# A two-layer decoder step: fewer page copies ahead of a weight load, one sum two tiles later, and a feed stage's first instructions reordered

## The chip, the cores and the metric

The kernel runs on one core of a Trainium2 chip. The metric is the device time of one execution in microseconds, as the median of several runs. The engines are PE (the matrix engine, with its weight loads as PEld), DVE (vector), ACT (activation), POOL (GpSimd) and SP, which issues most of the transfers.

## The reference, cut to what matters

Two layers of a decoder for a prompt group (16 meta tokens and 1024 prompt tokens) and a sample group (8 sequences of 4 tokens with 2048 past positions in a paged cache). The width is 1024.

```python
for i in range(2):
    n_p, n_s = rmsnorm(hp, norm_mix[i]), rmsnorm(hs, norm_mix[i])
    if i == 0:   # latent attention, 8 heads
        c_past = cache_kv_latent[0, page_table]     # 8 x 16 pages of 128 x 256
        kp_past = cache_k_rope[0, page_table]       # 8 x 16 pages of 128 x 64
        y_p = mla_output(mla_prompt_attend(...), w_kv_b, w_o)
        y_s = mla_output(mla_sample_attend(..., c_past, kp_past), w_kv_b, w_o)
    else:        # RWKV-7 time mixing
        y_p, y_s = rwkv7_time_mix(...)
    hp, hs = hp + y_p, hs + y_s
    hp = hp + sq_relu_mlp(rmsnorm(hp, norm_ffn[i]), ffn_w_up[i], ffn_w_down[i])
    hs = hs + sq_relu_mlp(rmsnorm(hs, norm_ffn[i]), ffn_w_up[i], ffn_w_down[i])

def rmsnorm(x, g):
    return x * rsqrt(mean(x * x) + eps) * g
```

## The kernel before, in words

The program is written engine by engine, each with its instructions in a fixed order; semaphores are counted. Activations lie with the features on the partitions, as `hT` (8 tiles of 128 features by 1072 tokens). Products in full precision are made of rounded high parts and remainders: ACT rounds an operand to its `hi` part, POOL (for weights) or DVE (for activations) subtracts to get the `lo` part, and PE multiplies hi by hi, hi by lo and lo by hi.

**Attention over the prompt, and the page copies (about 116 to 492 us).** The eight heads are worked in four pairs. Each pair has its own query and key-value weights in the tiles `wq`, `wqp` and `wkv`, which the next pair overwrites. When PE has made its last use of a pair's weights, in the second head, it raises `wkv_used` behind a drain (line 943); after the last scores of that head it waits for the next pair's weights on `wq_s` (the raw queries of the next pair). SP issues these weights in `load_pair` (three transfers of `mla_w_q_b`, one of `mla_w_kv_b`, line 1823). SP also copies the 128 pages of the cache that the page table names into the scratch tensor `past_scratch`, one page for each turn of a loop (`gather`, line 1873): it reads the page's number, computes addresses and issues two transfers. Ahead of the weights of pairs 2, 3 and 4 and behind the last stand 32 such copies each. The sample attention, which begins after the four pairs, reads the scratch tensor and waits for all 128.

**The start of each feed stage (about 651 to 790 us, and 2413 to 2565 us).** The tokens are in four quarters of 268. PE makes the output product of the mixer, tile by tile (8 tiles a quarter, in `added`, each into one of four banks of the ring BV), DVE adds each tile to `hT` (`adds`, line 3316) and so empties the bank. For the norm, ACT squares a quarter (`squares_at`, line 2710), POOL folds its eight tiles of squares into one (`fold`, lines 2184 and 2186), PE sums over the partitions with a matrix of ones (`sums_at`), ACT takes the root (`deviations_at`, line 2716), DVE takes the reciprocal (`roots`, line 3586) and scales (`scaled`, line 3593, eight instructions). The fourth quarter's squares come in pieces of 4, 3 and 1 tiles. In both layers the third quarter's sum stands on PE after tile 2 of the fourth quarter.

The feed product itself is a fast scheme with seven products of blocks of weights (A11, S2, S3, S1, A12, A22, S4; S are sums or differences of blocks) with blocks of activations (11, T2, T3, T1, 21, T4, 22), for two halves s of the tokens: s = 0 holds quarters 0 and 1, and s = 1 holds quarters 2 and 3. ACT rounds activation blocks in `round_block` (line 2725) and weights in `round_weights` (lines 2734 and 2740); DVE makes activation remainders in `split` (line 3608), and adds the products up in `second_sum`, `third_sum`, `out_22` and so on (line 3613). POOL makes the weight remainders (line 2214). In the first layer the tiles of the first weights lie where the output weights lie that PE is still reading; ACT and POOL may write them only when all 32 tiles of the output product are made. ACT gets there by standing behind the last square, POOL by waiting until DVE has emptied the last bank (`v_drained`). In the second layer these weights are prepared before.

## Time and profile before

| | |
|---|---|
| time, median of 3 runs | 3243.04 us (3242.75 to 3243.59) |
| the profiled execution's own time | 3241.11 us |
| its span | 3239.3 us |
| PE busy | 3092.5 us (95%) |
| DVE, ACT, POOL busy | 1881.9, 1357.9, 1261.1 us |
| chain that ended last | PE 70%, DVE 11%, PEld 5%, POOL 3%, ACT 3%, issue 3%, SPq 2%, DMA 1% |
| mean granted clock of PE | 0.989 |

The span runs from the first instruction to the last; 1.8 us of the execution lie outside it. The chain is followed back from the last instruction, at each step to what released it. SPq is SP's sequencer, that is, the time in which it works on transfers.

### The profile page before, as it was taken

Reading aid. Unit: us, or ns where it says so; the run is one execution under the profiler, and the core shown is the slowest. Engines: PE = TensorE matmul, PEld = TensorE weight load, DVE = VectorE, ACT = ScalarE, POOL = GpSimd, SP = SyncE. Lnnn points to the kernel's source line nnn. Section 1 sums busy time; section 2 is a strip of 40 time slices with the busy share of each in tenths; the row PEclk is TensorE's granted clock in tenths of the full one; section 3 lists DMA queues with packets and bytes.
Section 4 is the critical chain, followed back from the end, with each engine's and each line's share of the span. In section 5 each row is a group of like instructions: output and inputs, shape, how many; then the busy total and the mean of one; then the engine's idle time right before and its main releaser. Section 6 shows DMA issues by size and latency. Waiting matters only on the chain.

```text
span 3239.3 us, 70229 instructions
## 1 busy us (share of the span) xinstructions
PE 3092.5 (95%) x25828; PEld 2856.7 (88%) x25828; DVE 1881.9 (58%) x3193; ACT 1357.9 (42%) x2823; POOL 1261.1 (39%) x877
## 2 busy tenths in 40 slices
PE   8989999998999999999999999999999999999998
PEld 8778887797999999998899878787887899999998
DVE  5656663256444587765412577777735644458885
ACT  4334445424544433322223455655522454443332
POOL 0000000015766777732232122232224476677771
PEclk9999999999999999999999999999999999999999
DMA  3222225401544544431223201001151254454442
GB/s 115 60 80 75 70 60 176 151 14 57 163 157 158 180 138 142 141 98 58 78 80 116 74 21 46 28 27 34 43 174 33 75 161 159 157 175 147 147 133 78
DMA packets 307311, 330.49 MB, mean 102 GB/s; under 512 B 54366, under 2 KB 289809, under 8 KB 306994
## 3 DMA queue, kind: packets, MB, share of 16 engines
q1 hardware_dynamic: 301166, 308.54, 29.9%
q0 software_dynamic: 5904, 19.21, 1.9%
q8 instruction: 133, 2.18, 0.3%
q14 instruction: 56, 0.46, 0.0%
q10 hardware_dynamic: 52, 0.10, 0.0%
HBM read 232.05 MB, written 116.16 MB: 107 GB/s over the span
## 4 chain that ended last, share of the span: by engine, by line
PE 70%; DVE 11%; PEld 5%; POOL 3%; ACT 3%; issue 3%; SPq 2%; DMA 1%; PEldq 0%; DVEq 0%; ACTq 0%; POOLq 0%
PE bank L685 67%; PEld bank L685 5%; PE bank L693 4%; DVE arena L3926 1%; SPq L1873 1%; DVE hT L3997 1%; POOL wloA L2214 1%; DVE arena L3593 1%; POOL arena L2214 1%; DVE x_mix L3880 1%; DVE arena L3604 1%; POOL wloS L2214 1%; DMA arena<-in_mla_w_qkv_a 1%; DVE arena L3304 1%; SPq L1823 0%
## 5 line engine op out<-in xcount | busy, mean ns | idle before, releaser
L685 PE MATMUL bank<-arena 64*128 64x128 f32 (+19 forms) x6718 | 775.3, 304 | 40.7 <-DVE hT L3997 12.9
L685 PEld LDWEIGHTS bank<-arena 128*128 128x128 f32 (+9 forms) x6718 | 605.7, 162 | 177.0 <-issue 43.8
L2461 ACT COPY arena<-bank 128x512 f32<-128x512 f32 (+14 forms) x518 | 230.4, 484 | 599.9 <-PE bank L685 390.0
L2740 ACT ACTIVATE whiS<-arena 128x512 fp32r<-128x512 f32 x180 | 113.0, 628 | 404.9 <-POOL arena L2214 391.8
L2214 POOL TENSOR_TENSOR wloA<-arena,whiA 128x512 fp32r<-128x512 f32 x180 | 261.7, 1469 | 15.5 <-ACT whiA L2734 15.5
L2214 POOL TENSOR_TENSOR wloS<-arena,whiS 128x512 fp32r<-128x512 f32 x180 | 241.9, 1359 | 49.1 <-ACT whiS L2740 49.1
L2214 POOL TENSOR_TENSOR arena<-arena 128x512 f32<-128x512 f32 x120 | 165.8, 1382 | 229.2 <-PE bank L685 229.2
L3795 DVE TENSOR_TENSOR hT<-hT,bank 128x536 f32<-128x536 f32 x280 | 197.5, 706 | 82.4 <-PE bank L685 82.0
L693 PE MATMUL bank<-table,arena 128*128 128x128 f32 (+5 forms) x1422 | 181.0, 268 | 27.9 <-DVE arena L3476 13.1
L685 PE MATMUL bank<-hiT,whiS 128*128 128x268 f32 x768 | 198.8, 287 | 7.1 <-DVE fb L3608 3.8
L3613 DVE TENSOR_TENSOR arena<-std,bank 128x268 f32<-128x268 f32 x192 | 80.3, 431 | 214.6 <-PE bank L685 209.4
L693 PEld LDWEIGHTS bank<-table,arena 128*128 128x128 f32 (+5 forms) x1422 | 146.0, 135 | 54.0 <-issue 40.5
L2184 POOL TENSOR_TENSOR arena<-arena 128x536 f32<-128x536 f32 (+3 forms) x18 | 39.1, 2174 | 344.4 <-ACT arena L2710 314.0
L3736 DVE TENSOR_TENSOR arena<-arena 128x268 f32<-128x268 f32 x224 | 140.5, 668 | 41.5 <-ACT arena L2778 39.1
L685 PEld LDWEIGHTS bank<-hiT,whiS 128*128 128x128 f32 x768 | 145.1, 189 | 8.9 <-DVE fb L3608 4.2
L3316 DVE TENSOR_TENSOR hT<-hT,bank 128x268 f32<-128x268 f32 (+2 forms) x120 | 55.0, 468 | 167.7 <-PE bank L685 167.3
L3880 DVE SCALAR_TENSOR_TENSOR x_mix<-arena,prm 128x384 f32<-128x384 f32 (+1 forms) x96 | 57.8, 675 | 149.4 <-PEq L1280 149.1
L2207 POOL TENSOR_TENSOR q<-arena,q 64x1072 fp32r<-64x1072 f32 x4 | 9.8, 2451 | 325.5 <-ACT q L2602 325.5
L685 PE MATMUL bank<-hi,whiA 128*128 128x268 f32 x512 | 133.0, 288 | 3.3 <-DVE fb L3608 2.1
L685 PE MATMUL bank<-fb,whiA 128*128 128x268 f32 x512 | 132.3, 287 | 0.0
L685 PE MATMUL bank<-loT,whiS 128*128 128x268 f32 x512 | 132.1, 287 | 0.0
L685 PE MATMUL bank<-x_hi,w_hi 128*128 128x384 f32 (+1 forms) x384 | 127.0, 331 | 5.2 <-DVE x_lo L3887 3.2
(356 smaller groups left out, 8992.2 us busy)
## 6 DMA issues: line engine op xcount, KB each, us to landing
u_scratch<-arena SPq DMA_DIRECT2D x480, 134.0 KB, 1.8
arena<-in_ffn_w_up SPq DMA_DIRECT2D x64, 512.0 KB, 4.1
arena<-u_scratch SPq DMA_DIRECT2D x56, 536.0 KB, 4.9
arena<-in_ffn_w_down SPq DMA_DIRECT2D x112, 256.0 KB, 3.8
arena<-u_scratch SPq DMA_DIRECT2D x56, 402.0 KB, 5.6
arena<-past_scratch SPq DMA_DIRECT2D x32, 640.0 KB, 7.1
past_scratch<-in_cache_kv_latent SPq DMA_DIRECT2D x128, 128.0 KB, 2.4
past_scratch<-in_cache_k_rope SPq DMA_DIRECT2D x128, 32.0 KB, 2.1
```

The source lines that it names most:

```text
L685: return pe.matmul(out, lhsT, rhs, start=first, stop=last, skip_group_check=group)
L693: return pe.transpose(out, src, ident[0:rows, 0:rows])
L1873: sp.dma_start(dst, src).then_inc(gather_s, 16)
L2184: lane.do(pool.tensor_tensor(sq[:, 0:n, :], sq[:, 0:n, :], sq[:, n:2 * n, :], ALU.add))
L2214: return pool.tensor_tensor(out, a, b, op)
L2461: lane.do(act.copy(dst, b if view is None else view(b)), ring.drained)
L2740: ins = act.activation(hi[name][:, :, :], src, ACT.Copy)
L3316: lane.do(dve.tensor_tensor(hT[:, k, at:at + w], hT[:, k, at:at + w], b[:, 0:w], ALU.add), ring.drained)
L3613: dve.tensor_tensor(out, to, (BV, BA)[s][CHAIN[i]][:, 0:TS], ALU.add).then_inc(to_dve_b[layer].sem, 1)
L3736: dve.tensor_tensor(f.us[q, s], f.us[a, s], f.us[b, s], op).then_inc(diff_b[layer].sem, 1)
L3795: ins = dve.tensor_tensor(to[i], to[i], made, ALU.add)
L3880: ins = dve.scalar_tensor_tensor(out=x_mix[:, k, at:at + w], in0=DX[:, k, at:at + w], scalar=prm[:, k, R_MU + row:R_MU + row + 1], in1=nT[ ...
```

## The change

There are five edits. (1) The page copies ahead of the weights of pairs 2, 3 and 4 and behind the last are 27, 33, 34 and 34 instead of 32 each. (2) On PE, in both layers, the third quarter's sum stands after tile 4 of the fourth quarter instead of tile 2; on DVE the addition of tile 4 goes ahead of that quarter's root and scaling. (3) In the first layer ACT rounds weight A11 ahead of the last square, as soon as PE has made the last tile (`v_filled`), and takes the fourth quarter's deviation after S2 instead of after A22; in the second layer it takes it before rounding T4. (4) In the first layer POOL's first remainders wait for the last tile to be made instead of added. (5) DVE takes the fourth quarter's reciprocal ahead of the split of 21 in the first layer, and between the splits of 21 and T4 in the second.

```diff
--- before.py
+++ after.py
@@ -739,7 +739,7 @@
                         if (q, k) == (2, 2):
                             sums_at(layer, 0, (0, KT), ra.bank())
                             sums_at(layer, 1, (0, KT), ra.bank())
-                        if (q, k) == (3, 2):
+                        if (q, k) == (3, 4):
                             sums_at(layer, 2, (0, KT), ra.bank())
                 sums_at(layer, 3, (4, 7), last)
                 sums_at(layer, 3, (7, KT), last)
@@ -1877,11 +1877,12 @@
             load(rope_p, ctok[0:QT, 0:NQ, KVL:KVL + ROPE], out_t)
             load(O["lat_s"].rearrange("a b s n -> (a b s) n"), ctok_new[0:ND, 0:KVL], out_t)
             load(O["rope_s"].rearrange("a b s n -> (a b s) n"), ctok_new[0:ND, KVL:KVL + ROPE], out_t)
+            copied = (0, 27, 60, 94, DB * NPG)
             for i in range(1, H // 2):
-                gather((i - 1) * 32, 32)
+                gather(copied[i - 1], copied[i] - copied[i - 1])
                 sp.wait_ge(wkv_used, i)
                 load_pair(i)
-            gather(96, 32)
+            gather(copied[-2], copied[-1] - copied[-2])
             sp.wait_ge(out_s, out_t.n)
             sp.wait_ge(gather_s, 32 * DB * NPG)
             wv_t, wo_t = Tally(wv_s), Tally(wo_s)
@@ -2286,7 +2287,7 @@
                 fold_quarter(2)
                 fold_quarter(3, (0, 4))
                 if layer == 0:
-                    pool.wait_ge(v_drained, mark["adds0"] + 4 * KT)
+                    pool.wait_ge(v_filled, mark["adds0"] + 4 * KT)
                     first_splits()
                     fourth(0, None, unused)
                 weights_of(1, None, after_group(0, FIRST))
@@ -2819,17 +2820,23 @@
                 squares_at(3, (0, 4))
                 deviations_at(2)
                 squares_at(3, (4, 7))
+                if layer == 0:
+                    act.wait_ge(v_filled, adds + 4 * KT)
+                    round_weights(0, "A11", unused)
                 squares_at(3, (7, KT))
                 if layer == 0:
-                    for name in ("A11", "S3", "S2", "S1"):
+                    for name in ("S3", "S2"):
                         round_weights(0, name, unused)
+                    deviations_at(3)
+                    round_weights(0, "S1", unused)
                 round_block("21", 0)
                 if layer == 0:
                     round_weights(0, "A12", unused)
+                else:
+                    deviations_at(3)
                 round_block("T4", 0)
                 if layer == 0:
                     round_weights(0, "A22", unused)
-                deviations_at(3)
                 first_term(0, FIRST, 0, None)
                 round_block("22", 0)
                 if layer == 0:
@@ -3688,13 +3695,16 @@
                 adds(3, 1)
                 split(0, 2, "T3")
                 split(0, 3, "T1")
-                adds(3, 2, 3)
+                adds(3, 2, 3, 4)
                 roots(2)
                 scaled(2)
-                adds(3, 4, 5, 6, 7)
+                adds(3, 5, 6, 7)
+                if layer == 0:
+                    roots(3)
                 split(0, 4, "21")
+                if layer == 1:
+                    roots(3)
                 split(0, 5, "T4")
-                roots(3)
                 second_sum(0, FIRST, 0)
                 third_sum(0, FIRST, 0)
                 scaled(3)
```

On ACT, at the end of the fourth quarter in the first layer, before. (`arena<-hT` is a square, `std<-bank,eps` the deviation, `whi...` a weight's and `hi...` an activation block's rounded part.)

```order
L2710 ACTIVATE arena<-hT 128x3x268
L2710 ACTIVATE arena<-hT 128x268
L2734 ACTIVATE whiA11_0<-arena 128x512
L2740 ACTIVATE whiS3_0<-arena 128x512
L2740 ACTIVATE whiS2_0<-table 128x512
L2740 ACTIVATE whiS1_0<-arena 128x512
L2725 ACTIVATE hi21_0<-arena 128x4x268
L2734 ACTIVATE whiA12_0<-arena 128x512
L2725 ACTIVATE hiT4_0<-arena 128x4x268
L2734 ACTIVATE whiA22_0<-arena 128x512
L2716 ACTIVATE std<-bank,eps 128x268
```

And with the change:

```order
L2711 ACTIVATE arena<-hT 128x3x268
L2735 ACTIVATE whiA11_0<-arena 128x512
L2711 ACTIVATE arena<-hT 128x268
L2741 ACTIVATE whiS3_0<-arena 128x512
L2741 ACTIVATE whiS2_0<-table 128x512
L2717 ACTIVATE std<-bank,eps 128x268
L2741 ACTIVATE whiS1_0<-arena 128x512
L2726 ACTIVATE hi21_0<-arena 128x4x268
L2735 ACTIVATE whiA12_0<-arena 128x512
L2726 ACTIVATE hiT4_0<-arena 128x4x268
L2735 ACTIVATE whiA22_0<-arena 128x512
```

A11 moves ahead of the square of the last tile, and the deviation ahead of five of the roundings.

On DVE, from the third quarter's root in the first layer, before. (`hT<-hT,bank` is the addition of a tile, RECIPROCAL a root's, `fb0` and `loT4_0` are remainders, and `std<-std,bank` and `arena<-std,bank` are the second and third sum.)

```order
L3316 TENSOR_TENSOR hT<-hT,bank 128x268 x2
L3586 RECIPROCAL std<-std 128x268
L3593 SCALAR_TENSOR_TENSOR arena<-hT,prm,std 128x268 x8
L3316 TENSOR_TENSOR hT<-hT,bank 128x268 x4
L3608 TENSOR_TENSOR fb0<-arena,hi21_0 128x4x268
L3608 TENSOR_TENSOR loT4_0<-arena,hiT4_0 128x4x268
L3586 RECIPROCAL std<-std 128x268
L3613 TENSOR_TENSOR std<-std,bank 128x268
L3613 TENSOR_TENSOR arena<-std,bank 128x268
L3593 SCALAR_TENSOR_TENSOR arena<-hT,prm,std 128x268 x8
```

And with the change:

```order
L3323 TENSOR_TENSOR hT<-hT,bank 128x268 x3
L3593 RECIPROCAL std<-std 128x268
L3600 SCALAR_TENSOR_TENSOR arena<-hT,prm,std 128x268 x8
L3323 TENSOR_TENSOR hT<-hT,bank 128x268 x3
L3593 RECIPROCAL std<-std 128x268
L3615 TENSOR_TENSOR fb0<-arena,hi21_0 128x4x268
L3615 TENSOR_TENSOR loT4_0<-arena,hiT4_0 128x4x268
L3620 TENSOR_TENSOR std<-std,bank 128x268
L3620 TENSOR_TENSOR arena<-std,bank 128x268
L3600 SCALAR_TENSOR_TENSOR arena<-hT,prm,std 128x268 x8
```

One addition has moved ahead of the first reciprocal, and the second reciprocal ahead of both splits.

On PE, after tile 2 of the fourth quarter in the first layer. (`bank<-arena,table` is the sum with the matrix of ones.)

```order
 L685 MATMUL bank<-out_hi,wo_lo 128x268 x7
 L685 MATMUL bank<-arena 128x268
-L685 MATMUL bank<-arena,table 128x268
 L685 MATMUL bank<-out_hi,wo_hi 128x268
 L685 MATMUL bank<-out_lo,wo_hi 128x268
```

And after tile 4 of it:

```order
 L685 MATMUL bank<-out_hi,wo_lo 128x268 x7
 L685 MATMUL bank<-arena 128x268
+L685 MATMUL bank<-arena,table 128x268
 L685 MATMUL bank<-out_hi,wo_hi 128x268
 L685 MATMUL bank<-out_lo,wo_hi 128x268
```

The sum leaves the one place and stands at the other; the two tiles between them run first.

## Rows read from the trace of the kernel before

**Rows 1.** PE's own waits over the whole run: line, released by: total us, times, longest.

```profile
PE bank L685 <- DVE arena L3613: 10.1, 6, 4.5
...
PE bank L685 <- POOL arena L2186: 8.2, 2, 4.6
PE bank L685 <- DMA arena<-in_mla_w_kv_b: 6.7, 1, 6.7
```

**Rows 2.** timeline of SP's issues, 188 to 212 us: start, duration, engine, line, operation.

```profile
194.26 0.54 SPq L1873 DMA_DIRECT2D past_scratch<-in_cache_kv_latent  x1
...
206.80 0.54 SPq L1873 DMA_DIRECT2D past_scratch<-in_cache_kv_latent  x1
...
208.34 1.48 SPq L1823 DMA_DIRECT2D arena<-in_mla_w_q_b  x3
```

**Rows 3.** timeline of PE, 204 to 217 us; in brackets the idle time and its releaser.

```profile
206.38 0.43 PE L693 MATMUL bank<-table,arena 104*104 104x104 f32 x3
...
215.28 2.28 PE L685 MATMUL bank<-arena 128*128 128x384 f32 x3 [6.74 <-DMA arena<-in_mla_w_kv_b]
```

**Rows 4.** timeline of PE at the same place one pair of heads later.

```profile
313.67 0.43 PE L693 MATMUL bank<-table,arena 104*104 104x104 f32 x3
```

**Rows 5.** chain of waits, by time: start, us, what; the same piece of two pairs.

```profile
224.78 5.05 PE bank L685 x16
...
323.06 5.05 PE bank L685 x16
```

**Rows 6.** busy time by stretch: PE, PEld, DVE, ACT, POOL (x instructions), clock, DMA share, GB/s.

```profile
215.20:220.00 4.80, 4.72 (x9) 2.64 (x10) 0.48 (x1) 0.00 (x0) 0.00 (x0) 0.56 0.24 69
733.80:738.50 4.70, 4.68 (x24) 4.63 (x25) 0.00 (x0) 0.00 (x0) 0.00 (x0) 0.64 0.00 0
```

**Rows 7.** PE's drain at line 943: count, min/median/max ns, first and last start.

```profile
L943 PEldq DRAIN  x4: 1990/2043/2050, 186.7 to 490.2; - x4
```

**Rows 8.** timeline of SP's issues, 286 to 400 us: two weight loads, the last copy between.

```profile
296.09 1.46 SPq L1823 DMA_DIRECT2D arena<-in_mla_w_q_b  x3
...
385.57 0.56 SPq L1873 DMA_DIRECT2D past_scratch<-in_cache_kv_latent  x1
...
394.37 1.46 SPq L1823 DMA_DIRECT2D arena<-in_mla_w_q_b  x3
```

**Rows 9.** timeline of PE in the first feed stage, 725 to 741 us.

```profile
726.55 0.61 PE L685 MATMUL bank<-arena 128*128 128x268 f32 x2
...
729.58 0.61 PE L685 MATMUL bank<-arena 128*128 128x268 f32 x2
733.82 0.69 PE L685 MATMUL bank<-arena,table 128*128 128x268 f32 x2 [3.63 <-POOL arena L2186]
```

**Rows 10.** timeline of DVE in the first feed stage, 745 to 770 us.

```profile
751.68 0.43 DVE L3316 TENSOR_TENSOR hT<-hT,bank 128x268 f32<-128x268 f32 x1 [3.05 <-PE bank L685]
755.68 1.28 DVE L3608 TENSOR_TENSOR fb<-arena,hi 128x1072 fp32r<-128x1072 f32 x1 [3.56 <-ACT hi L2725]
...
761.64 6.42 DVE L3593 SCALAR_TENSOR_TENSOR arena<-hT,prm,std 128x268 f32<-128x268 f32 x8
```

**Rows 11.** timeline of ACT in the first feed stage, 745 to 770 us.

```profile
752.48 0.61 ACT L2734 ACTIVATE whiA<-arena 128x512 fp32r<-128x512 f32 x1
...
757.58 0.47 ACT L2716 ACTIVATE std<-bank,eps 128x268 f32<-128x268 f32 x1
```

**Rows 12.** timeline of POOL in the first feed stage, 745 to 770 us.

```profile
753.24 1.27 POOL L2214 TENSOR_TENSOR wloA<-arena,whiA 128x512 fp32r<-128x512 f32 x1 [10.29 <-ACT whiA L2734]
```

**Rows 13.** timeline of PE in the second feed stage, 2494 to 2512 us.

```profile
2494.44 11.11 PE L685 MATMUL bank<-arena 128*128 128x268 f32 x48 [0.25 <-DVE hT L3316]
2510.10 1.23 PE L685 MATMUL bank<-arena,table 128*128 128x268 f32 x2 [4.56 <-POOL arena L2186]
```

**Rows 14.** timeline of DVE in the second feed stage, 2470 to 2545 us.

```profile
2477.78 8.51 DVE L3593 SCALAR_TENSOR_TENSOR arena<-hT,prm,std 128x268 f32<-128x268 f32 x8
...
2530.86 0.43 DVE L3316 TENSOR_TENSOR hT<-hT,bank 128x268 f32<-128x268 f32 x1 [3.63 <-PE bank L685]
```

## The prediction

> **What bounds the kernel now.** I read the page first: PE is busy for 95% of the span and carries 70% of the chain that ended last, so a change of order gains only where PE stands still, or where the chain leaves PE. The second view is therefore the list of PE's own waits, over the whole run [rows 1]. Three of its lines stand where the change works. One wait of 6.7 us is for a transfer of `mla_w_kv_b`. Two waits, 8.2 us together, are for line 2186, POOL's fold of the squares. And the longest of all on DVE's line 3613, 4.5 us, stands in the first feed stage, where PE has run out of emptied banks. The third view is the timeline around each, where the reader is to see what the late thing itself was waiting for.
>
> **Part 1, the page copies.** SP starts its 27th copy at 194.26 and its 32nd at 206.80, so a copy costs it 12.54/5 = 2.51 us; the weights are issued at 208.34, 1.54 us after the last copy began [rows 2]. PE had allowed them long before: its first drain at line 943 starts at 186.7 and takes 2.0 us, so `wkv_used` stood at 188.8 [rows 7]. SP was late by its own work, and PE paid 6.74 us for it [rows 3]. With 27 copies the weights are issued at about 194.26 + 1.54 = 195.8, and land 12.5 us earlier than before, at about 202.7 where they landed at 215.3. PE asks for them at about 208.5, so the wait goes whole, with 5.8 us to spare.
>
> The gain is more than the wait. The same transposes stand at 206.38 in the first pair and at 313.67 in the second, 107.29 us apart [rows 3, 4], while a piece after the wait stands at 224.78 and 323.06, 98.28 us apart [rows 5]. The second pair has no such wait, so the stand costs 107.29 - 98.28 = 9.01 us: 6.74 of waiting and 2.27 of slower products behind it. The rows show why: after the stand PE runs for 4.8 us at a granted clock of 0.56, mostly the lower of its two levels, 1.2 and 2.4 GHz [rows 6]. I take 9.0.
>
> Beside this the Trainium skill speaks against counting so exactly: in "TensorE: Matmul & The Clock Gate", Part 1, it says that the slow stretch after idleness varies from run to run, and advises not to fit it. By that the second part of this gain, and the same part of two gains below, may not come; that is a rival below, with its price from the rows.
>
> What the 5 copies do elsewhere: they are spread, 1 more ahead of pair 3's weights, 2 more ahead of pair 4's, 2 more behind them. Allowances come every 98.28 us. Ahead of pair 4 the whole round between two weight loads, 32 copies and the loads, ended with the last copy starting at 385.57, when 296.09 was its start; that is 89.5 us, some 2.8 a copy, and SP then waited until 394.37 [rows 8]. Two more copies cost 5.6 us of those 8.8 us less the 1.5 us that the last copy takes: 1.7 us are left. Should SP come late after all, PE feels it only beyond the time from allowance to need (208.5 - 188.8 = 19.7 us) less issue and landing (7 us). So I cost this at nothing; its cover is 1.7 + 12.7 = 14 us. Behind pair 4's weights the two copies cost 5 us; the next allowance is due at 490.2 + 2.0 - 9.0 = 483.2 us [rows 7], and SP, at 394.37 - 9.0 + 3 + 34 x 2.6 = 477, is there before it.
>
> **Part 2, the third quarter's sum.** In the first layer PE ends tile 2 of the fourth quarter at 729.58 + 0.61 = 730.19 and stands 3.63 us until POOL's fold is done; tiles cost 3.03 us each before [rows 9]. The stretch from 733.8 on again has a low clock, 0.64 [rows 6]. Tile 7 is added at 751.68 [rows 10]. With two tiles between, PE reaches the sum at 736.3, 2.5 us after the fold is done. Each tile needs the bank of the one four back, whose addition lies some 9 us behind, so I count no wait for banks. PE goes on: 730.19 + 4 x 3.03 + about 0.4 for the third quarter's sum + 3.48 for tile 7 and the first sum of the fourth quarter (3.05 + 0.43, rows 10 have both) = 746.2. That is 5.5 us earlier: 3.6 of waiting, the rest clock.
>
> In the second layer the wait is 4.56 us; three tiles take 11.11 us, 3.62 each beyond the tail, and end at 2505.55 [rows 13]. Tile 7 is added at 2530.86, 4.06 us after the one before it [rows 14]. With the change: 2505.55 + 4 x 3.62 + 0.4 + 4.06 = 2524.5, 6.4 us earlier. What DVE does behind it is the same work in another order (the reciprocal between two splits, whose operands are there), with no POOL work beside it, so all 6.4 us should pass down to where PE is the bound again.
>
> The price of a later sum is a later root of the third quarter. Its sum ran at 733.82 and would now run at 736.3. But on DVE the root stands behind tile 3's addition, and that tile came only after PE's stand, at about 738; now tiles 3 and 4 are both made by 736.3, and the root is no later than before. It costs nothing.
>
> **Part 3, the reordering in the first feed stage.** From the last addition (751.68) to the fourth quarter's scaling (761.64) DVE needed 10.0 us: 0.4 for the addition, 3.56 of waiting for ACT's rounding of block 21, and from 755.68 on 5.96 us for five instructions, two splits, the reciprocal and two sums [rows 10]. ACT had rounded A11, S3, S2 and S1 first, from 752.48, and took the deviation last, at 757.58 [rows 11]. Now, counted from tile 7's end at 746.2: A11 (0.5), the last square (0.4), S3 and S2 (1.0), the deviation (0.5), so the reciprocal starts at 748.7, and while it runs (1.8 us) ACT gets through S1 and 21. The same five instructions then end at 748.7 + 5.96 = 754.7. Against 761.64 that is 7.0 us: 5.5 from part 2, and 1.5 of its own. POOL's first remainder, which began at 753.24, when ACT's A11 was ready [rows 12], begins at about 746.8; the waits on POOL that remain on PE are shorter than DVE's path. From the scaling on, DVE's work is what the products of both halves wait for (line 3613 again [rows 1]), so the 7.0 stand. A second A11 instruction ahead of the last square delays PE's last sum by 0.1 us, which nobody waits for.
>
> A bound for this part: DVE's eight scaling instructions took 6.42 us there [rows 10] and 8.51 us in the second layer, where POOL was at work all through [rows 14]. If POOL's earlier remainders now lie beside all of it, 2.1 us are lost; below, if it lies beside less, up to 2 us are won. The Trainium skill ("GPSIMD Engine Reference", Key points) says that the two engines share their way to SBUF and clash where a DVE instruction reads two tensors there, as the scaling does; it speaks for the worse end. I take no difference, as POOL keeps its distance: it was 6.4 us earlier, DVE 7.0.
>
> **The sum.** 9.0 + 7.0 + 6.4 = 22.4 us. The profiled execution took 3241.1 us and would take 3218.7. It stood 1.9 us under the median, so from 3243.0 I predict **3220.6 us**. No later stage is tied to the clock on the wall: past 800 us all transfers are released by engines.
>
> **The rivals.**
> - *The clock is not won back.* Then only the waits go: 6.74, 3.63 + 1.5 and 4.56, together 16.4 us, 3226.6 us. Against it: 107.29 - 98.28 is a difference of two places in one run. 7%.
> - *DVE and POOL clash.* The splits double as well as the scaling: 2.1 + 1.5 us lost, and a wait of like size on PE for the remainders; 3224 to 3225 us. 8%.
> - *The copies fall behind*, slower than before. It needs a copy to cost more than 2.8 us ahead of pair 4, as the copies and the weights share the transfer engines; with the 14 us of cover PE begins to wait at 2.8 + 14/34 = 3.2 us a copy. To be slower than before by 0.2% it would take 29 us of waiting, which is 4.0 us a copy. The worst pace in the rows is 2.8. 2%.
> - *The gain of the feed stages is given back* to a wait that the trace hides, say PE's for POOL's fourth weight sum, and only part 1 stands: 3234 us. 4%.
>
> **How the numbers follow.** The forecast has 79%, and a range of its own of 3217 to 3224: 2.1 us for the scaling either way, and some 1.5 us for the median. The range over all takes in the first two rivals: 3217 to 3227. A measurement of this kernel can tell about 0.2%, 6.5 us, from no change. All cases but the third lie beyond that on the fast side: faster 0.97, same 0.01, slower 0.02.
>
> **What would show it.** In the profile after, PE has no wait for `mla_w_kv_b` and the first pair is as long as the others; SP's last copy ahead of pair 4's weights starts just before PE allows them. The two waits for line 2186 are gone. In the first feed stage tile 7 is made 5.5 us earlier and the scaling of the fourth quarter starts 7 us earlier; if the two numbers are alike, part 3 brings nothing. In the second everything from tile 7 on is 6.4 us earlier. I am wrong if a stretch between these places has become longer, above all the page loads of the sample attention from 483 us on.

## The result and the profile after

| | before | after |
|---|---|---|
| median of the runs (lowest to highest) | 3242.89 us (3242.10 to 3243.59, 4 runs) | 3218.78 us (3217.26 to 3220.64, 4 runs) |
| ratio, 95% interval | | 0.9926 [0.9909, 0.9943] |
| profiled execution: time, span | 3241.1, 3239.3 us | 3217.26, 3215.5 us |

The changed kernel is faster by 24.1 us, 0.74%; forecast were 22.4 us. The predicted 3220.6 us is 1.8 us above the median, inside the range.

The work is the same, so I read the two traces against each other in one way throughout: the start of one and the same matmul in the trace of before, less its start in the other trace, taken at chosen places (the n-th matmul of one is the n-th of the other). I call this number the **lead**. Where it jumps, time was won or lost; where it stays, nothing was. It is worked out from the start times in the traces; the table further down has it for every kernel but e4, which has 104 matmuls more.

First the pairs. The list of PE's waits of the changed kernel over the whole run (total us, times, longest):

```profile
PE bank L685 <- DVE arena L3620: 9.8, 6, 4.5
...
PE bank L685 <- POOL wloS L2215: 7.7, 5, 1.7
```

The wait for `mla_w_kv_b` and the two for POOL's fold, all three in [rows 1], are gone from the list. Line 3620 here is line 3613 of before; its 9.8 us and the 4.5 us one stayed. Timeline of SP's queue in the changed kernel (start, us, queue, line, operation, how many), and of PE around the place of the old wait:

```profile
193.24 0.55 SPq L1873 DMA_DIRECT2D past_scratch<-in_cache_kv_latent  x1
...
194.78 2.82 SPq L1823 DMA_DIRECT2D arena<-in_mla_w_q_b  x3
197.64 0.49 SPq L1823 DMA_DIRECT2D arena<-in_mla_w_kv_b  x1
...
208.53 0.55 PE L693 MATMUL bank<-table,arena 104*104 104x104 f32 x4
208.91 6.85 PE L685 MATMUL bank<-arena 128*128 128x384 f32 x26
```

The 27th copy starts at 193.24, the weights at 194.78 (w_q_b) and 197.64 (kv_b) where they stood at 208.34 and later [rows 2], and the matmuls at 208.91 follow the one at 208.53 with no wait, where [rows 3] had 6.74 us. The window behind it (busy us of each engine with counts, the granted clock, DMA share, GB/s):

```profile
215.20:220.00 4.80, 4.80 (x24) 3.34 (x23) 4.32 (x6) 0.74 (x2) 0.00 (x0) 1.00 0.24 68
```

and the chain of waits (start, us, what) at the two points of [rows 5]:

```profile
216.30 5.05 PE bank L685 x16
...
314.57 5.05 PE bank L685 x16
```

The clock is 1.00 where it was 0.56 [rows 6], and the same piece comes 98.27 us after itself. The lead goes from -0.5 to 8.5 us here: 9.0.

Now the first feed stage. The timeline of the changed kernel from tile 7's addition on, DVE, then one row of ACT and one of POOL:

```profile
736.15 0.43 DVE L3323 TENSOR_TENSOR hT<-hT,bank 128x268 f32<-128x268 f32 x1 [3.05 <-PE bank L685]
738.54 1.83 DVE L3593 RECIPROCAL std<-std 128x268 f32<-128x268 f32 x1 [1.95 <-ACT std L2717]
740.28 1.62 DVE L3615 TENSOR_TENSOR fb<-arena,hi 128x1072 fp32r<-128x1072 f32 x1
741.82 2.37 DVE L3615 TENSOR_TENSOR loT<-arena,hiT 128x1072 fp32r<-128x1072 f32 x1
...
744.92 6.66 DVE L3600 SCALAR_TENSOR_TENSOR arena<-hT,prm,std 128x268 f32<-128x268 f32 x8
751.50 1.26 DVE L3615 TENSOR_TENSOR fb<-arena,hi 128x1072 fp32r<-128x1072 f32 x1
...
736.15 0.63 ACT L2735 ACTIVATE whiA<-arena 128x512 fp32r<-128x512 f32 x1 [2.14 <-PE bank L685]
...
736.92 1.28 POOL L2215 TENSOR_TENSOR wloA<-arena,whiA 128x512 fp32r<-128x512 f32 x1 [9.86 <-ACT whiA L2735]
```

Tile 7 is added at 736.15 (751.68 before [rows 10]), the reciprocal starts 2.39 us behind it, and the scaling at 744.92, 8.77 us behind tile 7 where it was 9.96. The splits, though, took 1.62 and 2.37 us, and the scaling 6.66 where [rows 10] have 6.42. In the second stage tile 7 is added at 2509.25 (before 2530.86 [rows 14]), again with no wait on POOL:

```profile
2509.25 0.43 DVE L3323 TENSOR_TENSOR hT<-hT,bank 128x268 f32<-128x268 f32 x1 [3.63 <-PE bank L685]
...
2516.03 3.35 DVE L3600 SCALAR_TENSOR_TENSOR arena<-hT,prm,std 128x268 f32<-128x268 f32 x8
```

The lead rises by 5.4 us up to tile 7 of the first stage, by 1.0 from there to 765 us, and by 6.3 in the second stage. That makes 9.0 + 5.4 + 1.0 + 6.3 = 21.7 of the 23.8 us between the spans. The rest stands at places that differ between executions of one kernel (last section): -0.5 ahead of the change, +1.6 at the start of the first feed stage, +0.4 between 765 and 1000, -1.6 between 1100 and 1200, and +2.2 behind 2900 us.

### The profile page after: what moved, and what is told of

It is laid out like the page before. It is cut to its first block, busy times and chain, and to the rows that moved or that the text cites. A ratio compares the mean times of both kernels' runs of the same rounds, so it can differ in the third digit from the quotient of the medians.

```text
span 3215.5 us, 70230 instructions
## 1 busy us (share of the span) xinstructions
PE 3085.3 (96%) x25828; PEld 2853.0 (89%) x25828; DVE 1880.4 (58%) x3193; ACT 1358.9 (42%) x2823; POOL 1261.7 (39%) x877
## 4 chain that ended last, share of the span: by engine, by line
PE 74%; DVE 10%; PEld 5%; POOL 3%; ACT 3%; issue 2%; DMA 1%; PEldq 0%; DVEq 0%; SPq 0%; ACTq 0%; POOLq 0%
PE bank L685 70%; PEld bank L685 5%; PE bank L693 4%; DVE arena L3936 1%; DVE hT L4007 1%; POOL wloA L2215 1%; POOL arena L2215 1%; DVE arena L3600 1%; DVE x_mix L3890 1%; POOL wloS L2215 1%; DMA arena<-in_mla_w_qkv_a 1%; DVE arena L3311 1%; DVE arena L3471 1%; DVE arena L3953 0%; DVE x_lo L3897 0%
## 5 line engine op out<-in xcount | busy, mean ns | idle before, releaser
L685 PE MATMUL bank<-arena 64*128 64x128 f32 (+19 forms) x6718 | 770.7, 303 | 33.9 <-DVE hT L4007 12.9
L685 PE MATMUL bank<-fb,whiS 128*128 128x268 f32 x512 | 132.3, 288 | 0.0
```

The source lines that it names most:

```text
L685: return pe.matmul(out, lhsT, rhs, start=first, stop=last, skip_group_check=group)
```

## The experiments

All twelve, with the kernel before run beside them in each of three groups. Medians first, since the later argument rests on the leads: the groups' medians of before were 3242.99 (21 runs), 3243.54 (11) and 3243.84 us (8).

| kernel | median us (runs) | ratio [95%] |
|---|---|---|
| e1_copies_only | 3234.97 (6) | 0.9968 [0.9956, 0.9981] |
| e2_sum_only | 3227.78 (4) | 0.9948 [0.9931, 0.9964] |
| e3_reorder_only | 3242.54 (10) | 0.9996 [0.9986, 1.0007] |
| e4_busy_wait | 3242.06 (10) | 0.9995 [0.9986, 1.0005] |
| e5_a11_late | 3226.94 (5) | 0.9944 [0.9931, 0.9956] |
| e6_deviation_late | 3219.30 (5) | 0.9928 [0.9915, 0.9941] |
| e9_outputs_first | 3221.58 (5) | 0.9929 [0.9916, 0.9942] |
| after_again | 3223.32 (6) | 0.9933 [0.9916, 0.9951] |
| e7_three_more_copies | 3219.01 (4) | 0.9924 [0.9908, 0.9941] |
| e8_eight_more_copies | 3233.12 (5) | 0.9966 [0.9951, 0.9980] |
| e11_one_tile_later | 3220.60 (4) | 0.9924 [0.9907, 0.9940] |
| e10_second_layer_too | 3221.20 (4) | 0.9931 [0.9914, 0.9948] |

The lead in us, at places given by the time in the trace of before (205 and 228: ahead of and behind the first pair's old wait; 428: behind pair 4's weights; 670: inside the first feed stage; 728 and 745: ahead of and behind the moved sum; 765: behind the scaling; 1000: far behind that stage; 2500 and 2530: around the moved sum of the second layer):

```
                       205   228   428   640   670   728   745   765  1000  1200  1860  1910  2340  2430  2500  2530  3230
after                 -0.5   8.5   8.5   8.5  10.1  10.1  15.5  16.5  16.9  15.3  15.2  15.2  15.2  15.3  15.3  21.6  23.9
after_again            1.3  10.3  10.3   9.0  10.5  10.5  15.9  16.9  16.8  16.8  14.2   9.8   9.8   9.3   9.3  15.6  15.6
e1_copies_only         0.1   9.1   9.1   7.7   9.2   9.2   9.2   9.2   9.1   9.2   9.3   4.9   4.9   4.3   4.3   3.6   3.8
e2_sum_only            1.1   3.2   3.3   1.8   3.3   3.2   8.7   8.6   8.9   8.6   7.2   7.2   7.2   7.2   7.2  13.5  14.7
e3_reorder_only        0.3   2.0   2.0   0.5   3.6   3.6   2.5   3.5   3.9   3.6   2.3   2.3   2.3   2.3   2.3   2.3   2.9
e5_a11_late            0.7   9.7   9.7   8.4   9.8   9.8  15.2  15.5  15.8  15.5  13.2   8.9   8.9   6.5   6.5  12.8  14.5
e6_deviation_late      1.2  10.2  10.2  11.9  13.5  13.5  18.9  19.4  20.0  20.0  17.4  17.4  17.4  17.1  17.1  23.4  23.4
e9_outputs_first       0.9   9.9   9.9   8.8  10.2  10.2  15.6  18.3  16.7  16.6  13.7  12.1  12.1  10.9  10.9  17.2  19.5
e7_three_more_copies  -0.8   8.2   8.2   7.0   8.4   8.4  13.8  14.7  14.7  14.8  14.1  14.1  13.8  12.7  12.7  19.0  21.2
e8_eight_more_copies   1.4  10.4   0.3   2.0   3.6   3.6   9.0  10.0  10.3   9.4   9.8   9.8   9.6   8.3   8.3  14.6  16.1
e11_one_tile_later    -0.3   8.8   8.7   7.4   8.8   8.8  13.3  14.3  14.8  14.7  12.1   7.7   7.4   5.0   4.9  10.1  10.6
e10_second_layer_too  -0.4   8.6   8.6   7.1   8.5   8.5  13.9  14.9  14.9  14.5  13.9  13.9  13.9  11.2  11.2  17.5  18.6
```

Every kernel with part 1 gains 9.0 us between 205 and 228, every one with part 2 gains 5.4 between 728 and 745 and 6.3 between 2500 and 2530 (e11 less, by design). Part 3 shows between 745 and 765: 0.96 or 0.97 us in the seven traces that have the whole of it and nothing moved behind it, and 0.01 at most in e1 and e2, which have none. The other jumps are the executions' own (last section).

Every row is taken against one and the same trace of before. That the jumps agree to 0.1 us shows how well the changed places repeat. It does not show that the kernel before always loses that much there, and it does not: e2 and e3 still have the first wait, and yet are 2.2 and 1.7 us ahead of it between 205 and 228. The section on the clock comes back to this.

### Each part alone

**e1_copies_only.** Part 1 alone, on the kernel before:

```
-                gather((i - 1) * 32, 32)
+                gather(copied[i - 1], copied[i] - copied[i - 1])     # copied = (0, 27, 60, 94, 128)
```

> The kernel before with the page copies alone changed (27, 33, 34, 34). My theory: the wait for the weights of pair 2 goes, and the slow stretch behind it: 9.0 us less. Rival, only the wait goes: 6.7 us less. Rival, the two extra copies ahead of the weights of pair 4 and behind them make SP late: less than 6 us, with a new wait on PE for mla_w_kv_b or for the page loads.

The median is 8.0 us lower; the lead jumps by 9.0 at the place, 6.74 of it the wait. The rival in which the slow products stay is out by the trace; the median, with an interval from 6.2 to 14.3 us, cannot tell 6.7 from 9.0.

**e2_sum_only.** Part 2 alone:

```
-                        if (q, k) == (3, 2):
+                        if (q, k) == (3, 4):
```

with DVE's `adds(3, 2, 3)` and `adds(3, 4, 5, 6, 7)` cut as in the change.

> The kernel before with the third quarter's sum alone moved, in both layers, and the addition of tile 4 ahead of that quarter's root on DVE. My theory: 5.5 us from the first feed stage and 6.3 us from the second, 11.8 us less; tile 7 of the fourth quarter is made that much earlier and everything behind it with it. Rival, only the waits go, 3.6 and 4.6: 8.2 us less. Rival, DVE gives it back in the first stage, since the later root delays it: 6.3 us less.

The median is 15.2 us lower, with an interval of the ratio that reaches from 11.7 to 22.4 us; the lead says 5.4 and 6.3, together 11.7. Its profiled execution is 14.7 us ahead at the end, and the other 3.0 us stand at places that the edit does not touch. The scaling starts 9.97 us behind tile 7, as before, so nothing of part 3 comes with it.

**e3_reorder_only.** Part 3 alone: POOL's first remainder on the earlier semaphore, ACT's and DVE's new order.

> The kernel before with the reordering of ACT, POOL and DVE alone (A11 ahead of the last square, the fourth quarter's deviation and reciprocal earlier, POOL's wait on v_filled), the sum and the copies as before. My theory: from tile 7 of the fourth quarter to the fourth quarter's scaling 8.5 us instead of 10.0 in the first feed stage: 1.5 us less, and nothing in the second. Rival, POOL's work falls beside more of DVE's: 0 us. In time this is near what the runs of one kernel differ by; the profile decides.

The median cannot tell it from nothing (0.45 us). In the trace the scaling starts 8.76 us behind tile 7 (9.96 before) and the next split 15.34 us behind it (16.30 before). The lead rises by 0.97 us between 745 and 765. The 1.1 us that it loses at the sum come from slower products. PE's timeline of e3 around the stand, the same last row in before, and e3's window behind the stand (granted clock third from the end):

```profile
725.97 0.61 PE L685 MATMUL bank<-arena 128*128 128x268 f32 x2
730.22 1.23 PE L685 MATMUL bank<-arena,table 128*128 128x268 f32 x2 [3.64 <-POOL arena L2186]
...
735.94 0.62 PE L685 MATMUL bank<-arena 128*128 128x268 f32 x2
```

```profile
738.47 0.61 PE L685 MATMUL bank<-arena 128*128 128x268 f32 x2
```

```profile
730.20:736.00 5.80, 5.78 (x24) 5.58 (x25) 0.00 (x0) 0.00 (x0) 0.00 (x0) 0.50 0.00 0
```

The stand is 3.64 us, as it was (3.63). But from the end of tile 2 to the end of the tile behind the sum it is 735.94 - 725.97 = 9.97 us, where before had 738.47 - 729.58 = 8.89 [rows 9]: the clock was at its lower level, 0.50, for all of the 5.8 us, where [rows 6] have a mean of 0.64.

### Does the clock really come back?

**e4_busy_wait.** The kernel before, with products of ones with ones in place of the stand:

```
+                if q == 2:
+                    for _ in range(26):
+                        mm(b[:, 0:P], ones, ones[:, 0:P], True, True)
```

> The kernel before, with 26 products of a table of ones by itself put on PE ahead of the third quarter's sum in each layer, into the bank that the sum then overwrites, so that PE works for some 3.2 us of the time that it stood still. It adds nothing to the result. My theory that 1.6 us of each stage's gain is the clock: the products behind the sum run at the high level, and each stage is 1.2 to 1.8 us shorter than before, 3 us less in all, though PE reaches the sum no earlier. Rival, the slow stretch has another cause: the time is that of before, or up to 1 us longer.

The median is 0.9 us lower, less than expected and less than it can tell. PE's timeline of this kernel at the two sums:

```profile
726.83 0.61 PE L685 MATMUL bank<-arena 128*128 128x268 f32 x2
727.28 5.97 PE L685 MATMUL bank<-table 128*128 128x128 f32 x52
733.08 0.62 PE L685 MATMUL bank<-arena,table 128*128 128x268 f32 x2
...
2511.51 0.62 PE L685 MATMUL bank<-arena,table 128*128 128x268 f32 x2
2511.96 14.62 PE L685 MATMUL bank<-arena 128*128 128x268 f32 x64
```

and the same place in the second layer of the kernel before:

```profile
2511.13 15.63 PE L685 MATMUL bank<-arena 128*128 128x268 f32 x64
```

The filling products took 5.97 us, too long for stands of 3.63 and 4.56: from one tile's sum to the third quarter's it is 6.25 us where before had 733.82 - 729.58 = 4.24 [rows 9]; in the second layer the sum came 16.75 us behind the start of the three tiles, 15.66 before. That loses 2.0 and 1.1 us. But the 64 products behind the sum take 14.62 us where they took 15.63, and the sum itself 0.62 where [rows 13] have 1.23: 1.6 us won back, and in the first stage likewise (the tile behind it ends 9.29 us behind the row at 726.83; before, 738.47 - 729.58 = 8.89, so of the 2.0 lost 1.6 came back). The clock went with it (same columns as above, at the two sums):

```profile
733.00:738.00 5.00, 5.00 (x40) 4.86 (x39) 0.43 (x1) 0.76 (x1) 0.00 (x0) 1.00 0.02 3
2511.00:2527.00 16.00, 16.00 (x75) 13.56 (x75) 6.69 (x13) 1.47 (x2) 2.06 (x2) 1.00 0.00 0
```

So in these two traces the clock's part of either stand is 1.6 us, as I had expected, and it goes when PE is merely kept busy. The expectation of 3 us less failed on the length of the filling.

**The clock's part is not the same each time.** That came out of the other traces. Four kernels still have the first wait (before, e2, e3, e4), and three the stands at the sums (before, e1, e3). The first wait was 6.74, 5.04, 5.33 and 5.35 us in before, e2, e3 and e4, and the 26 products behind it took 8.96, 8.48, 8.68 and 9.63 us, where 6.85 is the time without a stand. All in all that stand cost 9.0, 6.8, 7.3 and 8.3 us, 1.8 to 2.9 of it behind the wait. The stand of the first feed stage cost 1.1 us more in e3 than in before and e1. The one of the second layer (4.55 or 4.56 us) cost 0.7 us more in e1 than in before and e3, where the 64 products took 15.63 and 15.65; e1's timeline:

```profile
2506.79 16.37 PE L685 MATMUL bank<-arena 128*128 128x268 f32 x64
```

What decides it is open. So 9.0, 5.4 and 6.3 us are the gains over one execution of the kernel before; over another one they would have been up to 2.2 us less or up to 1.1 us more at a place.

### Which half of part 3?

**e5_a11_late** and **e6_deviation_late** each undo one half of part 3 in the changed kernel. e5 rounds A11 behind the last square and has POOL wait for `v_drained` again; e6 puts the deviation and the reciprocal back:

```
-                if layer == 0:
-                    act.wait_ge(v_filled, adds + 4 * KT)
-                    round_weights(0, "A11", unused)
                 squares_at(3, (7, KT))
                 if layer == 0:
-                    for name in ("S3", "S2"):
+                    for name in ("A11", "S3", "S2"):        # e5
```
```
-                if layer == 0:
-                    roots(3)
                 split(0, 4, "21")
-                if layer == 1:
-                    roots(3)
                 split(0, 5, "T4")
+                roots(3)                                    # e6
```

> The changed kernel, with A11 of the first feed stage rounded behind the last square again, and POOL's first remainder waiting for the later semaphore; the earlier deviation and reciprocal stay. Theory (DVE sets the pace there, and what part 3 brings comes from the deviation alone): POOL's first remainder starts about 1 us later than in the changed kernel (736.92), PE's wait for it in front of the first product grows from 0.34 to about 1.2 us, the fourth quarter's scaling still starts 8.8 us after tile 7's addition, and the time is 0 to 0.3 us more. Rival (the early A11 is what brought the gain): the products of the whole stage are 1.0 us or more later, 1.0 to 1.5 us more in all.

> The changed kernel, with the fourth quarter's deviation behind all roundings on ACT and its reciprocal behind both splits on DVE again, in the first layer; A11 stays early. Theory: the scaling starts 1.5 us later than in the changed kernel, 10.3 us after tile 7's addition where it was 8.8, everything behind it in the first feed stage is 1.5 us later, and the time 1.5 us more. Rival (the early A11 brought it): the scaling starts no more than 0.5 us later and the time is the same.

DVE in e5, then in e6 (tile 7's addition, the scaling, the next split):

```profile
736.45 0.43 DVE L3320 TENSOR_TENSOR hT<-hT,bank 128x268 f32<-128x268 f32 x1 [3.05 <-PE bank L685]
...
745.95 6.65 DVE L3597 SCALAR_TENSOR_TENSOR arena<-hT,prm,std 128x268 f32<-128x268 f32 x8
752.52 1.26 DVE L3612 TENSOR_TENSOR fb<-arena,hi 128x1072 fp32r<-128x1072 f32 x1
```

```profile
732.80 0.43 DVE L3320 TENSOR_TENSOR hT<-hT,bank 128x268 f32<-128x268 f32 x1 [3.05 <-PE bank L685]
...
743.24 5.39 DVE L3597 SCALAR_TENSOR_TENSOR arena<-hT,prm,std 128x268 f32<-128x268 f32 x8
748.55 1.26 DVE L3612 TENSOR_TENSOR fb<-arena,hi 128x1072 fp32r<-128x1072 f32 x1
```

From tile 7 to the split behind the scaling it is 16.07 us in e5, 15.75 in e6, 15.35 in the changed kernel and 16.30 before. So A11 ahead of the last square (with POOL's earlier semaphore) is worth 0.72 us. 0.47 of it is that A11's rounding fills the time in which ACT waits for PE's last sum, and in e5 stands ahead of the deviation; the rest is a split that POOL holds up for longer (1.88 us instead of 1.62). The theory, that the scaling would start 8.8 us behind tile 7 without it, failed: it starts 9.50 behind. The deviation ahead of the rounding of block 21 is worth 0.40 only: in e6 the scaling does start 1.67 us later (10.44 us behind tile 7, 8.77 in the changed kernel), as expected, but it then takes 5.39 us where it took 6.66, since POOL, at its remainders since 733.57, is further on. The lead says the same: from 745 to 765 it rises by 0.96 us in the changed kernel, by 0.23 in e5 and by 0.55 in e6. Neither theory nor rival had that: the halves are both real, and the larger is the one that I had as a side effect. Of the medians e5's is 8.2 us above the changed kernel's, but 4.4 of this fall at 1860 to 1910 and 2.4 at 2340 to 2430 in its profiled execution, which the edit does not touch.

**e10_second_layer_too.** `roots(3)` and `deviations_at(3)` forward in the second layer as well.

> The changed kernel, with the deviation and the reciprocal of the fourth quarter put forward in the second layer too, as in the first. Theory (DVE waits 1.48 us there for ACT's rounding of block 21, and would wait as long for the deviation, since both stand behind PE's last sum): the scaling starts 0 to 0.3 us earlier or later after tile 7's addition (6.78 us in the changed kernel), the same time. Rival (the rounding runs beside the reciprocal and its wait goes): 1.0 to 1.5 us earlier.

```profile
2513.32 0.43 DVE L3322 TENSOR_TENSOR hT<-hT,bank 128x268 f32<-128x268 f32 x1 [3.63 <-PE bank L685]
...
2520.51 3.35 DVE L3599 SCALAR_TENSOR_TENSOR arena<-hT,prm,std 128x268 f32<-128x268 f32 x8
```

The scaling starts 7.19 us behind tile 7 instead of 6.78, so it is 0.4 us worse: no A11 is to be rounded there, ACT rounds block 21 while PE makes the last sum, and the split can start before the reciprocal.

### Where the sum has to stand

**e11_one_tile_later.** `(q, k) == (3, 3)` in place of `(3, 4)`.

> The changed kernel with the third quarter's sum one tile later than before (behind tile 3) where the change puts it two tiles later, in both layers. Theory: PE comes 0.6 us too early for POOL's fold in the first layer and 0.9 us in the second, and so short a stand doesn't bring the clock down: 1.5 us more than the changed kernel. Rival (any stand there costs the clock too): 1.6 us on top in each layer, 4.7 us more.

PE's waits, whole run:

```profile
PE bank L685 <- POOL arena L2187: 1.6, 2, 1.0
```

The two stands are 1.6 us together, as worked out. The lead gains 4.5 and 5.1 where two tiles gain 5.4 and 6.3: one tile gives 2.1 us less, 1.6 of waiting and 0.5 more. The clock is not lost again. The median, 3220.6, cannot show so little.

### What DVE bounds behind it

**e9_outputs_first.** The addition that frees the bank for which PE waits 4.53 us, ahead of the scaling, in both layers:

```
-                scaled(3)
                 split(0, 6, "22")
                 out_22(0, FIRST, 0)
+                scaled(3)
```

> The changed kernel, with the split of block 22 and the addition that empties its bank (five quarter-blocks' worth, about 2 us of DVE) ahead of the fourth quarter's scaling on DVE, in both layers. Theory (DVE's work, not the bank, is the bound behind that place): PE's wait of 4.53 us for line 3620 falls to under 1 us, but the scaling starts 1.7 us later, and PE waits that much longer for the second half's splits; the time is 0 to 3.5 us more for the two layers together. Rival (PE's wait for the bank is a loss of its own): 3 to 8 us less.

```profile
751.35 0.36 PE L685 MATMUL bank<-hi,whiS 128*128 128x268 f32 x1 [1.97 <-issue]
...
755.75 0.36 PE L685 MATMUL bank<-hi,whiA 128*128 128x268 f32 x1 [2.69 <-DVE fb L3615]
```

PE's 4.53 us for line 3620 are gone; in their place stand 1.97 and 2.69, and the scaling starts at 746.69, 10.58 us behind tile 7 instead of 8.77. The lead rises by 6.5 us between 728 and 1000, where the changed kernel's own two traces have 6.8 and 6.3, and by 6.3 in the second layer, as there. So nothing is won and nothing lost. The wait was only where the work of DVE showed on PE.

### How much room the copies have

**e7_three_more_copies** and **e8_eight_more_copies**: `copied = (0, 30, 60, 94, 128)` and `(0, 27, 60, 102, 128)` in the changed kernel.

> The changed kernel with 30 page copies ahead of the second pair's weights where it has 27. Theory (PE had 5.8 us to spare, as predicted, and a copy costs SP 2.51 us): the weights are issued 7.5 us later, and PE waits 1.7 us for mla_w_kv_b (1.5 to 2.5, if the landing takes somewhat longer); the time is 2 to 4.5 us more, the upper end if the clock falls behind so short a stand too. Rival (copies and weights share the transfer engines, and what counts is not the order on SP): no wait, the same time.

> The changed kernel with 42 page copies ahead of the fourth pair's weights where it has 34. Theory (14 us of cover as predicted: SP's own slack, 2.0 us in the changed kernel's profile, and 12.7 us between PE's allowance and PE's need): SP is 18.8 to 21 us late for the allowance, PE waits 6 to 8 us for the fourth pair's weights, and about 2.3 us go to the slower clock behind it; the time is 8 to 10 us more. Rival (the cover is longer or shorter than I worked out): a wait under 4 or over 10 us.

```profile
200.59 0.54 SPq L1873 DMA_DIRECT2D past_scratch<-in_cache_kv_latent  x1
...
202.14 1.49 SPq L1823 DMA_DIRECT2D arena<-in_mla_w_q_b  x3
203.67 0.49 SPq L1823 DMA_DIRECT2D arena<-in_mla_w_kv_b  x1
...
209.17 6.85 PE L685 MATMUL bank<-arena 128*128 128x384 f32 x26
```

```profile
404.25 1.49 SPq L1823 DMA_DIRECT2D arena<-in_mla_w_q_b  x3
...
411.52 9.00 PE L685 MATMUL bank<-arena 128*128 128x384 f32 x26 [7.82 <-DMA arena<-in_mla_w_kv_b]
```

In e7 three copies put the 30th at 200.59, 7.35 us later, but kv_b's transfer follows at 203.67, only 6.03 us later, since the three of w_q_b ahead of it took 1.49 us to issue and not 2.82. By its semaphore it landed at 208.84, 5.17 us behind its issue, and PE takes it at 209.17 without a wait. In the changed kernel it landed at 201.64, 3.99 us behind its issue, and PE took it at 208.91. So the rival's figure came true, not its reason: the room was 7.3 us, and the landing, 7.20 us later, just fitted. In e8 the first of the loads is issued at 404.25, 20.3 us behind the allowance, and PE waits 7.82 us: the cover from allowance to need is 12.5 us (forecast 12.7). The lead falls by 10.1 us, 2.3 more than the wait, the clock again. The median is 12.9 us above the changed kernel's ten executions, more than the 8 to 10 expected; the five executions spread from 3225.0 to 3236.5.

### The kernel again

**after_again.** The changed kernel unaltered.

> The changed kernel itself once more, to see how far its executions spread and whether POOL's stand of 7.35 us in the down-product stage stays at its place (1109.11 in the first trace). Expected: a median of 3217 to 3221 us; one such stand at another place, or none or two, and the time 1.8 to 2.2 us more or less for each.

The six executions took 3212.3 to 3232.2 us, and their median, 3223.3, lies above the 3217 to 3221 expected. With the four of the result the median of ten is 3220.3 us. The 24.1 us of the first set were a little lucky; the jumps of the lead at the changed places are the same in both traces to 0.1 us. The "stand of 7.35 us" on record was a misreading of mine; what it is stands in the last section.

## Why the prediction was right

**Part 1** was right in its mechanism, and in its numbers against the trace from which they were read: 9.0 us, 6.74 of waiting and 2.3 of clock, in each of the ten traces that have it. How much the kernel before loses there is less fixed: 6.8 to 9.0 us in the four traces that have the wait, 7.9 on average, and the medians gave 8.0 (e1). The spare was 7.3 us (5.8 forecast), the cover 12.5 (12.7), and SP waited 2.0 us ahead of pair 4 (1.7). Behind pair 4 SP's last copy starts at 472.05 and it then stands until the page loads at 483.82 (forecast 477 and 483.2), so the two copies there cost nothing.

**Part 2** gave 5.4 us (forecast 5.5) and 6.3 (6.4). No wait for a bank came, and the third quarter's reciprocal did not come late. Of the 1.8 us beyond the wait in each, e4 won 1.6 back by keeping PE busy; e3 and e1, which still have the stands, lose 1.1 and 0.7 us more at one of them.

**Part 3** was over-sized: the term "7.0 us: 5.5 from part 2, and 1.5 of its own". It measured 0.97 us (lead from 745 to 765, seven traces; none in e1 and e2). The step that failed was "the same five instructions then end at 748.7 + 5.96": they took 6.38, and the scaling took 0.24 more. I had named a clash with POOL as a bound for the scaling and taken no difference, "as POOL keeps its distance". In start times it nearly did: against tile 7 POOL's first remainder came 0.8 us earlier and the scaling 1.2. POOL was beside both splits before as well; what changed is how far POOL's remainder had come when a split was due. POOL and DVE at the second split before, then at both splits of the changed kernel (744.19 = 741.82 + 2.37 is the end of the second, in the result's rows):

```profile
755.71 2.38 POOL L2214 TENSOR_TENSOR wloS<-arena,whiS 128x512 fp32r<-128x512 f32 x1
757.19 2.04 DVE L3608 TENSOR_TENSOR loT<-arena,hiT 128x1072 fp32r<-128x1072 f32 x1 [0.24 <-ACT hiT L2725]
```

```profile
739.48 1.29 POOL L2215 TENSOR_TENSOR wloS<-arena,whiS 128x512 fp32r<-128x512 f32 x1
740.73 2.32 POOL L2215 TENSOR_TENSOR wloS<-arena,whiS 128x512 fp32r<-128x512 f32 x1
```

A split that starts while POOL is at an instruction ends 1.13 or 1.14 us behind the end of that one, so the two engines take turns here, an instruction at a time: 759.23 and 758.09 before, 741.90 and 740.77, 744.19 and 743.05 here. It holds for all 135 such splits of the fourteen traces; the other 257 take 1.2 to 1.3 us. The remainder of 740.73, in turn, is held up by the first split and takes 2.32 us instead of 1.29. So the first split took 1.62 us where it had come just as POOL finished and taken 1.28, the second 2.37 instead of 2.04, and of these 0.67 us DVE got back 0.24 that it had stood between them. The scaling is alike: an instruction of it that starts beside one of POOL's ends 0.3 us behind it and takes up to 1.5 us here, the others 0.5. The eight took 6.66 us here, where four met POOL, 5.39 in e6, where two did, and 3.35 in the second layer with POOL idle. What the Trainium skill says in "GPSIMD Engine Reference", Key points, that POOL and a DVE instruction reading two tensors clash, fits with these rows. The full clash of the rival (3224 to 3225 us) did not come. And what was found is mostly A11's, not the deviation's (e5, e6).

**The sum**: 9.0 + 5.4 + 1.0 + 6.3 = 21.7 us by the leads, against 22.4. From the medians, some 3243 us for before and 3220.3 for the ten executions of the changed kernel, it is 22.7. That the two agree with the forecast to 1 us is in part luck, since single executions of either kernel differ by 10 us and more. The rivals are out: the clock was won back, the copies did not fall behind, and nothing of the feed stages' gain was given back to POOL's fourth sum. The Trainium skill's warning ("TensorE: Matmul & The Clock Gate", Part 1) that the slow stretch varies from run to run is borne out in size: behind the first stand it cost 1.8 to 2.9 us, and at the other two it came out up to 1.1 us longer than in the trace that I had read. It did come at each of the eleven stands of 3.6 us and more that these traces have at these places (with the one of e8), so a forecast that left it out would have been wrong.

## What to carry to other kernels

A stand of PE costs its length and then some of the products behind it; two places of one trace that do the same work, one with the stand and one without, give both parts at once, for that trace, and moving a consumer past one or two independent tiles wins both. When two engines share work around a place, making both earlier does not keep them as they were: see at which point of the one's instruction the other's now comes. Where single executions differ by more than the edit is worth, compare traces at fixed instructions; the medians here could tell neither part 3 nor e11 from nothing. And take more than one trace of the kernel before, since what it loses at a stand differs too.

## What the runs showed of the hardware

**A slow clock at a fixed place, by chance.** One group of 24 products in the second layer takes 2.94 us in nine profiled executions and 4.57 or 4.58 in five (after_again, e1, e5, e9, e11), never a value between. PE's timeline of the changed kernel, its first profile and then the second:

```profile
1862.25 2.94 PE L685 MATMUL bank<-arena 128*128 128x128 f32 x24 [0.69 <-ACT arena L3060]
```

```profile
1863.23 4.57 PE L685 MATMUL bank<-arena 128*128 128x128 f32 x24 [0.69 <-ACT arena L3060]
```

The window around these products in the second (granted clock third from the end):

```profile
1862.00:1866.00 4.00, 3.31 (x20) 3.18 (x20) 3.79 (x9) 0.60 (x1) 0.00 (x0) 0.72 0.00 0
```

The granted clock was 0.72 in those 4 us. The 1.6 us do not stay alone: DVE now meets POOL at other instructions. A copy of 8 columns takes 1.87 us (from 1878.40) instead of 0.17; it starts beside a POOL instruction that ends at 1880.24 and ends at 1880.27. And the lead falls by 4.4 us in four of the five. The start of the first feed stage behaves alike: between 428 and 670 us the lead stays (eight traces, to 0.3 us), or rises by 1.6 (after, e3) or 3.2 and 3.3 (e6, e8). What decides it is open. All five slow groups are in kernels with part 1, but so are five of the nine others, and four traces without it are too few to say that it can't happen there. A wait for the last of `rwkv_w_o` near 2370 us (0 to 1.8 us, then 64 products at up to 11.3 us instead of 9.6) comes and goes in the same way, in e4 too, which has no part of the change.

**Rounds of 41.6 us that are sometimes 43.2.** The down products go in rounds, and I first took a piece of the chain of waits, 7.35 us of "issue" beside POOL, for a stand of POOL's without a cause, since it stood at 1109.11 in one trace and at 3065 in the other. POOL's timeline at the first, with the instruction behind each such wait:

```profile
1116.49 1.29 POOL L2215 TENSOR_TENSOR arena<-arena 128x512 f32<-128x512 f32 x1 [6.33 <-PE bank L685]
...
1159.67 1.29 POOL L2215 TENSOR_TENSOR arena<-arena 128x512 f32<-128x512 f32 x1 [6.34 <-PE bank L685]
```

POOL waits once in every round for PE to leave a buffer, in all four traces that I followed (before, the changed kernel twice, e6): 6.3 to 6.6 us, which in itself nobody pays for. Whether the chain passes there differs. What differs is the length of a round: 41.57 us from 1201.24 to 1242.81, but 43.18 from 1116.49 to 1159.67, in which PE waited up to 1.7 us for one of POOL's remainders ("POOL wloS" in the list of PE's waits). The kernel before had two rounds of 42.57 us, from 2988.63 to 3031.20 and from 3072.74 to 3115.31, where the changed one has 41.55 in all; the changed one had its long round at 1116. That is the -1.6 and the +2.2 above. With the slow groups it makes the spread of single executions, 3212.3 to 3232.2 us of one kernel, nearly as large as the whole effect of this change.
